# Compression stage of a hybrid decoder step: positions on partitions, row-tiled first product, prompt in a shared job

## The reference, cut to what matters

```python
def _chunk_feats(rows, pe, w1):                 # rows (B, L, G, 64)
    c = rows.reshape(B, L // 16, 16, G, 64)
    pe2 = pe.reshape(2, 16, 1, 64); w = w1.reshape(2, 16, 64, 128)
    head = einsum('bnrge,ref->bngf', c + pe2[0], w[0])
    tail = einsum('bnrge,ref->bngf', c + pe2[1], w[1])
    return head, tail
compressed = einsum('bngf,fe->bnge', gelu(head[:, :-1] + tail[:, 1:]), w2)
```

## Time and profile before

| what | value |
|---|---|
| median of 3 runs | 2173.88 us (2154.34 to 2179.73) |
| the profiled execution, its own time | 2180.32 us |
| its span, first to last instruction | 2178.5 us |
| mean granted TensorE clock | 0.95 of full |
| PE busy | 88% of the span |
| DVE, ACT, POOL busy | 52%, 37%, 12% |
| stage `prepare` | 350.2 to 548.5 us, 198.3 us |

### The profile page before, as it was taken

The page is one execution under the profiler, slowest core; times in us unless marked ns, Lnnn a source line. Parts: engine busy times, 40 slices in busy tenths (PEclk is TensorE's granted clock), DMA queues, the critical chain, the costliest instruction groups (busy, mean ns, idle before and its releaser), DMA issues. The chain is left out here.

```text
span 2178.5 us, 30219 instructions
## 1 busy us (share of the span) xinstructions
PE 1916.3 (88%) x10675; PEld 1569.3 (72%) x10675; DVE 1132.0 (52%) x2682; ACT 815.3 (37%) x1727; POOL 264.1 (12%) x334
## 2 busy tenths in 40 slices
PE   3998996457788879899996799999999999999997
PEld 3787775456677667777775687788788878878885
DVE  4866860112566757777785433443443444344334
ACT  3444430100577656666664323221222122122211
POOL 0000000101333333433332000000000000000000
PEclk6998997788899989999998899999999999999999
DMA  5322213661455533223223421211220221123012
GB/s 179 104 93 81 80 55 58 89 120 27 128 143 144 153 78 98 78 82 109 80 83 94 157 78 58 97 59 39 97 84 24 86 97 59 39 97 111 28 36 86
DMA packets 172330, 189.96 MB, mean 87 GB/s; under 512 B 55942, under 2 KB 139110, under 8 KB 171000
## 3 DMA queue, kind: packets, MB, share of 16 engines
q1 hardware_dynamic: 170114, 187.13, 29.5%
q10 hardware_dynamic: 2080, 1.05, 0.2%
HBM read 166.60 MB, written 59.81 MB: 104 GB/s over the span
## 5 line engine op out<-in xcount | busy, mean ns | idle before, releaser
L2352 DVE SCALAR_TENSOR_TENSOR m_conv<-m_ext,m_taps,m_conv 128x512 f32<-128x512 f32 x44 | 33.1, 751 | 371.7 <-ACT m_ext L2244 371.7
L1603 ACT ACTIVATE l_e<-l_e,l_nmin 128x640 f32<-128x640 f32 (+11 forms) x224 | 169.5, 757 | 32.0 <-DVE l_nmin L1663 31.8
L2094 PE MATMUL o_py<-f_h_hi,m_gu_hi 128*128 128x512 f32 x704 | 179.9, 397 | 0.0
L2094 PE MATMUL o_py<-f_h_lo,m_gu_hi 128*128 128x512 f32 x704 | 178.5, 395 | 0.0
L2094 PE MATMUL o_py<-f_h_hi,m_gu_lo 128*128 128x512 f32 x704 | 178.5, 395 | 0.0
L1562 ACT ACTIVATE l_pT_hi<-l_t 128x512 fp32r<-128x512 f32 (+3 forms) x288 | 126.8, 470 | 128.7 <-PE l_t L1351 126.0
L1663 DVE CUSTOM_DVE_ANT_0 l_e<-l_s,k_masks 128x1024 f32<-128x1024 f32 (+3 forms) x192 | 138.0, 719 | 69.5 <-PE l_s L1311 64.1
L2242 ACT ACTIVATE m_conv<-o_py,m_taps 128x512 f32<-128x512 f32 (+1 forms) x66 | 42.8, 648 | 333.3 <-PE o_py L2094 333.3
L1738 DVE TENSOR_TENSOR l_pT_lo<-l_t,l_pT_hi 128x512 fp32r<-128x512 f32 (+3 forms) x288 | 143.6, 526 | 31.4 <-ACT l_pT_hi L1562 30.8
L1351 PE MATMUL l_t<-k_ident,l_e 128*128 128x128 f32 x816 | 134.2, 283 | 28.3 <-DVE l_pT_lo L1738 18.9
L2094 PEld LDWEIGHTS o_py<-f_h_lo,m_gu_hi 128*128 128x128 f32 x704 | 132.0, 187 | 32.3
(11 more groups left out here) (284 smaller groups left out, 3996.2 us busy)
## 6 DMA issues: line engine op xcount, KB each, us to landing
m_raw_gu<-in_w_gate SPq DMA_DIRECT2D x22, 512.0 KB, 5.6
m_raw_gu<-in_w_up SPq DMA_DIRECT2D x22, 512.0 KB, 6.8
m_raw_d<-in_w_down SPq DMA_DIRECT2D x11, 1024.0 KB, 5.1
p_raw<-in_w_in SPq DMA_DIRECT2D x5, 2048.0 KB, 8.0
c_rows<-in_cache_cmp SPq DMA_DIRECT2D x64, 128.0 KB
a_kd_k<-in_state_dil SPq DMA_DIRECT2D x8, 1024.0 KB, 8.0
a_kd_v<-in_state_dil SPq DMA_DIRECT2D x8, 1024.0 KB, 7.8
a_kd_k<-in_cache_slc SPq DMA_DIRECT2D x128, 64.0 KB, 1.8
```

The lines of the kernel that those rows point to most:

```text
L1603: nc.scalar.activation(e, e, ACT.Exp, bias=nmin[0:r, k:k + 1], scale=-1.0, accum_out=total[0:r, k:k + 1]).then_inc(exped, 1)
L2094: last = nc.tensor.matmul(bank[q % 3][:, 0:w], ws[k][:, m, c, :], hs[:, c, t0:t0 + w], start=(j == 0 and c == 0), stop=(j == 2 and c == KC ...
```

## The change

- **Rows with positions on partitions.** A page goes to 128 partitions, 1 KB on each (its 128 positions). 16 DMAs a job as before. POOL's copies and the buffer `rows16` are gone: PE transposes straight from `c_rows`. After a transpose one partition half holds head 0 and the other head 1, with positions along the columns.
- **First product in two row tiles.** For each of the 32 positions r of a window and each head g there is one matmul with 64 partitions (half g), weights 64 x 128, and moving data that takes every 16th column. Head 0 and head 1 go to different PSUM banks. w1 is loaded twice (once for each half), in 4 DMAs of 64 partitions instead of 2 of 128, and pe likewise.
- **Prompt in a shared job.** 4 jobs instead of 5; job 1 has the prompt as a third part beside its two samples (189 columns a matmul). The prompt's rows come by one DMA of their own behind the pages of job 1, and the kv result is stored in the middle of the block.
- **Encodings with w1 moving.** pe is the stationary operand (one column), w1 moves (128 columns): 64 matmuls in alternating halves into rows in `c_hidden`'s banks, copied by DVE to `bias_rows`, turned to columns by 4 small matmuls.
- **Turns two jobs ahead.** PE's order is now turn(0), turn(1), then for m: hid(m), project_kv(m-1), turn(m+2). Turning uses a ring of 3 banks (`RING`), there is one bank for the second product instead of 2.
- `c_k_new` is loaded ahead of the first pages; load_rows(m) waits for job m-2 to be turned. Buffers share memory (`p_xsq` with `p_zsq`; `u`, `kv` with `q_new`), and `a_kd_v` and `l_late` change place.

```diff
-            load_rows(0)
             for dst, src in zip((k_new[:, 0:512], k_new[:, 512:512 + P], k_new[:, 512 + P:]), new_k):
                 sp.dma_start(dst, src).then_inc(kn_in, 16)
+            sp.wait_ge(b.pages_in, 16)
+
+            def load_rows(m):
+                for i in range(2):
+                    for n in range(PAGES):
+                        sp.dma_start(rows[m % 2][:, i, n].rearrange("p c n -> p (c n)"),
+                                     t["cache_cmp"][bass.ds(ld.page(2 * m + i, n), 1)].rearrange("b p c g e -> (b p) (c g e)")).then_inc(rows_in[m % 2], 16)
+
+            load_rows(0)
...
             load_rows(1)
+            sp.dma_start(rows_p[:].rearrange("p a c n -> p a (c n)"),
+                         o["cmp_prompt"].rearrange("b s c g e -> (b s) (c g e)").rearrange("(a p) n -> p a n", p=P)).then_inc(rows_p_in, 16)
...
             for m in range(2, JOBS):
-                sp.wait_ge(rows_ready, 4 * (m - 1))
+                sp.wait_ge(t_filled, chunk(m - 1, 0))
                 load_rows(m)
...
+        def chunks_of(m):
+            return [(c, i, quad) for c in range(2) for i in range(parts(m)) for quad in range(2)]
...
             def hid(m):
...
                 for c in range(2):
-                    for j in range(16):
-                        at = j // 8
-                        if m < PROMPT:
-                            src = xT[m % 2][:, c, j % 8, :, :].rearrange("p g (b n) -> p (g b) n", n=NS)[:, :, at:at + NCMP]
-                        else:
-                            src = xT[m % 2][:, c, j % 8, :, at:at + NCMP]
-                        last = nc.tensor.matmul(hidden[m % 2][:, c, 0:n, 0:NCMP], w1[:, c, j, :], src, start=(j == 0), stop=(j == 15))
+                    for r in range(CMP_LEN):
+                        for g in range(GA):
+                            hp = slice(g * E, (g + 1) * E)
+                            x = xT[m % 2][hp, c, 0:parts(m), :].rearrange("p b (n r) -> p b n r", r=CMP_STRIDE)
+                            last = nc.tensor.matmul(hid_at(m, c, g), w1[hp, c, r, :], x[:, :, r // CMP_STRIDE:r // CMP_STRIDE + NCMP, r % CMP_STRIDE],
+                                                    start=(r == 0), stop=(r == CMP_LEN - 1))
                 last.then_inc(hid_done, 1)
...
+            encode_turn()
             turn(0)
+            turn(1)
             for m in range(JOBS):
                 hid(m)
-                if m + 1 < JOBS:
-                    turn(m + 1)
-                if m == 0:
+                if m == 1:
                     pe.wait_ge(pe_copied, 1)
-                project_kv(m)
+                if m >= 1:
+                    project_kv(m - 1)
+                if m + 2 < JOBS:
+                    turn(m + 2)
+            project_kv(JOBS - 1)
...
     for c, x in enumerate("kv"):
-        k.loads += [(k.w1[:, c], t["w1_cmp_" + x].rearrange("(j p) f -> p j f", p=P)), (k.w2[:, c], t["w2_cmp_" + x])]
+        for g in range(GA):
+            k.loads.append((k.w1[g * E:(g + 1) * E, c], t["w1_cmp_" + x].rearrange("(r e) f -> e r f", e=E)))
+        k.loads.append((k.w2[:, c], t["w2_cmp_" + x]))
```

More of the change, by code:

```diff
@@ L630, in prepare @@
         sem = lambda name: ctx.enter_context(nc.semaphore(name))
-        q_new = sb("c_q_new", [NS, 2, 512])
+        q_new = sb("c_q_new", [P, 2, 512])
         k_new = sb("c_k_new", [NS, 512 + 2 * P])
[L633 to L638, removed]
@@ L639, in prepare @@
[L639 to L642 removed]
+        rows = [sb(f"c_rows{k}", [P, 2, PAGES, 2, P]) for k in range(2)]
+        rows_p = sb("c_rows_p", [P, PAGES, 2, P])
+        xT = [sb(f"c_xT{k}", [P, 2, 2 + k, SEQ]) for k in range(2)]
@@ L651, in prepare, with parts @@
         block = ctx.enter_context(nc.Block())
+        def parts(m):
+            return 3 if m == PROMPT else 2
+        def chunks_of(m):
+            return [(c, i, quad) for c in range(2) for i in range(parts(m)) for quad in range(2)]
         first = 4
-        chunk = lambda m, n: first + 8 * m + n
-        def width(m):
-            return P if m < PROMPT else NS
+        chunk = lambda m, n: first + sum(len(chunks_of(x)) for x in range(m)) + n
         @block.sync
@@ L711, in _ @@
             nc.gpsimd.memset(b.bd_nsa[:], 0.0).then_inc(zeroed, 1)
[L712 to L719, removed]
+            pool.wait_ge(t_filled, 2)
+            nc.gpsimd.memset(kv, 0.0).then_inc(zeroed, 1)
         @block.tensor
@@ L775, in _, with encode_turn @@
+            def encode_turn():
+                pe.wait_ge(bias_copied, 1)
+                for c in range(2):
+                    for x in range(2):
+                        last = nc.tensor.matmul(small[:, c:c + 1], bias_rows[0:1, c, x, :], ident[0:1, 0:1], start=(x == 0), stop=(x == 1))
+                last.then_inc(bias_done, 1)
             pe.wait_ge(new_in, 48)
@@ L778, in _ @@
                 for j in range(4):
-                    last = nc.tensor.transpose(dst[:, j * NS:(j + 1) * NS], q_new[:, n, j * P:(j + 1) * P], ident[0:NS, 0:NS])
+                    last = nc.tensor.transpose(dst[:, j * NS:(j + 1) * NS], q_new[0:NS, n, j * P:(j + 1) * P], ident[0:NS, 0:NS])
                 last.then_inc(t_filled, 1)
[L781 to L784, removed]
+            encode()
             pe.wait_ge(kn_in, 48)
@@ L851, in _ @@
+            copy(pe_bias[:], small[:, 0:2]).then_inc(pe_copied, 1)
             ch.step(nc.vector.tensor_scalar(w2[:], w2[:], 0.5, None, ALU.mult))
-            dve.wait_ge(pe_copied, 1)
+            for n in range(0, len(chunks_of(1)), 2):
+                take(dve, copy, 1, n)
+            dve.wait_ge(gates_up, 2)
+            for g_ in (b.gate_p, b.gate_s):
+                ch.step(nc.vector.tensor_scalar(g_[:], g_[:], 1.0, None, ALU.add))
+                nc.vector.reciprocal(g_[:], g_[:])
@@ L863, in _ @@
                 nc.vector.tensor_tensor(y, y, x, ALU.mult).then_inc(tanh_in, 1)
-                if m + 1 < JOBS:
-                    for n in range(0, 8, 2):
-                        take(dve, copy, m + 1, n)
+                if m + 2 < JOBS:
+                    for n in range(0, len(chunks_of(m + 2)), 2):
+                        take(dve, copy, m + 2, n)
                 dve.wait_ge(tanh_done, m + 1)
@@ L1041, in attend @@
         sem = lambda name: ctx.enter_context(nc.semaphore(name))
+        late = sb("l_late", [P, 3 * SEQ], F32R)
         ident_r = sb("l_ident_r", [P, P], F32R)
```

178 lines of the change are left out of this document (95 added, 83 removed).

## The result

The changed kernel takes 2206.05 us in the median (2202.51 to 2210.1, 4 runs), the kernel before in the same series 2170.93 (2154.34 to 2179.73, 4 runs): a ratio of 1.0165, with a 95% interval of 1.0124 to 1.0205. It is slower, by 1.2 to 2.05%, so whether by over 2% stays open; 2130 was forecast with a range up to 2195.

The account below looks back on a forecast made before the run. Late cached rows from slow page loads were taken to bound the compression stage; -51 us there and +4 for w1 gave -47, from 2180.3 to 2133 or 2127 against the median, forecast 2130, range 2096 to 2195.

Parts of the forecast that it names:

- What bounds the stage: Compression stage: late cached rows from slow page loads on half the DMA engines; POOL only passes the delay to PE.
- The first product: Compression stage on PE: four jobs' products take 62.5 us in all at 1.72 ns a column, with full overlap.
- The overlap of the row tiles: First product: both row tiles run at once, a pair costing one 126-column matmul, 13.9 us a job; otherwise double.
- rival C: First product: strided moving read costs double; 2310 to 2320 us if tiles don't overlap, chance 0.08 for that unpaired case.
- Rival B: First product: row tiles don't overlap, 29.4 us a job, 2188 to 2194; chance 0.12 including the overlapped strided case.
- w1 twice: Block `project`: 2 MB more of w1 delays the first store 7 us; PE stall taken as 4 us, range 0 to 10.
- Rival A: First product: 128-column weight loads run one at a time, 27.4 us a job, 2168 to 2174; chance 0.20.
- Rival D: SP's queue in the stage: 1.35 us a page with backlog as before, 2145 to 2155; chance 0.10.
- The chain: SP's and PE's worked-out order through the compression stage: end at 497.5 instead of 548.5, a gain of 51 us.
- the wait ahead of turn(1): PE in the compression stage waits 20 us for the prompt's rows before turning job 1; its longest wait.
- Encodings: PE early in the stage: 13.7 to 27 us, free because hidden before job 1's rows arrive.
- one more wait at nothing: Turns of later jobs behind gelu on DVE: taken as hidden because the rows come no earlier, no cost.
- Sum: Whole kernel: 51 us gained in the stage, 4 lost to w1's loads, together -47; forecast 2130 us.

Follow-up runs that it names:

- the repaired kernel: Changed kernel with features stored by position first, w1 on 128 partitions and PE's order one job ahead: 2118.96 us, ratio to before 0.9726.

## Why the prediction was wrong, point by point

- **What bounds the stage** was read rightly. The loads, the half-used DMA engines and POOL as messenger were the bound; once pages went to 128 partitions PE's waits for the samples' cached rows are 7.9 us in all (it had waited 42.6 for POOL's copies of them), beside 24.2 for the prompt's; 16 pages took 17.3 us to issue where 17.6 was taken.
- **The first product: this step failed.** It took the price of a column, 1.72 ns, from a contiguous read and carried it over to a read of every 16th column. The overlap of the row tiles, which took all the weighing, is real (14.6 against 27.8 us); the column costs 3.4 ns. 124.6 instead of 62.5 us. The stride stood in rival C, whose overlapped half was put together with B at 0.12 and priced at 2188 to 2194. By the page "SBUF — State Buffer" of the Trainium skill, Door 1, crossing to a new 16-byte line at each access costs; here that is exactly the border (2 columns a line free, 1 column a line double), though its next sentence, by which 4 fp32 can be strided for free, is not what the run shows. No row of before has a strided moving operand; the place where I chose wrongly is that I then forecast at the price of the rows there were.
- **w1 twice: right mechanism, wrong size.** Half rate onto 64 partitions was the upper end (14 us later, a stall of 10); 4 was taken. Measured: store 14 us later, PE idle 13.4, the stage 15.0 later. The delay of the store was the upper end to the microsecond. The stall came out larger, since ACT's copy came only when the store had landed 5 us after its issue, and PE came back at 1.2 GHz. The mis-sized part is the rate onto 64 partitions; with w1 on 128 the stall is 4.0 us, the forecast's own number. Its "512 B packets" for w1 before was misread (0.73 MB in 362 packets, 2 KB each, in 58.5 to 61 us), without harm to the sum. The rule on ports of the Trainium skill's page "SBUF — State Buffer", Door 1, had spoken for the upper end, and the 128-partition loads (290 and 323 against 177 GB/s) agree with it.
- **Rival A** (weight loads one at a time) would give the same time for 126 and for 189 columns. It falls: 27.8 and 41.2, and 14.6 with contiguous columns, below the 27.4 that it allows. (Its 0.107 us a load is half of the 0.216 that rows 7 show at a granted clock of 0.50; no row shows it itself.)
- **Rival B** (no overlap) came near the product's time, 29.4 and 41.5, but by the wrong mechanism; the exchanged loops show it.
- **Rival D** (SP slower, 1.35 us a page): it falls with those 17.3 us.
- **The chain**, apart from these two terms, held: it gives 147.3 us for the stage with a product of full speed; the run with neighbouring columns has 151.2 (365.8 to 517.0), with the wait ahead of turn(1) at 23 us where 20 was worked out. Encodings were hidden as said (9.6 us). It put one more wait at nothing: turns 2 and 3 stand for DVE, which is at gelu, 2.3 and 2.7 us in the changed kernel (1.4 and 2.7 with neighbouring columns). What the chain saw and did not follow up is that wait: it was listed as PE's longest and taken as a cost of the loads, while it was one of PE's order, worth 18 us in the repaired kernel and 31 in the changed one.
- **Sum.** -47 was forecast. To it come 11 of w1 (15 for 4) and 62 of the product: +26, where the profiled spans show +22, with 4.6 less behind the stage that nothing explains. So the miss is these two terms. The medians show +35; the rest of that is the spread of the runs of before, 25 us. C's price was low by the same w1 term, which is why even B and C's end of the range, 2195, fell short of 2206.

## What to carry to other kernels

Price a matmul by its moving operand's address pattern as well as by its columns: where fp32 columns lie 16 B or more apart, let the engine that evacuates PSUM do the reordering, which cost nothing here. Before two totals are compared, compare the granted clock under them. Ask of each wait in a worked-out chain not only how long it is but what that engine already holds that it could do in it. And a constant loaded early is not free: look at what stands behind it in its queue, and spread it over all partitions (290 against 177 GB/s here).

## What the runs showed of the hardware

- At a granted clock of 1.00 TensorE's fp32 moving read cost double at strides of 4 and 16 columns (16 and 64 B): 14.7 and 13.9 us for 128 records, against 7.3 at stride 2 and for neighbouring columns.
- The strided read took the same time at both clock levels: about 0.21 us a record of one half at 1.00 (428.5 to 431.5 us) and at 0.50 (434 to 437 us), in the run with the loops exchanged. The clock fell between the two while PE ran record after record.
- Two 64-partition row tiles with 128-column weights, alternated matmul by matmul into different banks, run at once: 14.6 against 27.8 us, also at the strided price (0.108 against 0.21 us a record, both at a clock of 1.00).
- DVE and ACT read PSUM at a stride of 16 columns in fp32 at the contiguous price (0.69 and 0.60 us for 128 x 512).
- Loads of 512 B packets move 177 GB/s onto 64 partitions (w1 in the changed kernel) and 323 onto 128 (MLP weights in the kernel before).
- A DMA issue on ACT lasted 14 us with 2 MB issued just ahead of it, and ACT's next work waited behind it.
